# Two-block transformer kernel on one core: router's logits by token, halved refills, nine taps on TensorE, postponed GpSimd products

## The reference, cut to what matters

```python
def conv_mixer(...):                       # layer 0 of the first block
    u = x @ w_in; a_val, a_gate, b_b, b_c, b_x = split(u)
    a = a_val * sigmoid(a_gate)
    a = causal_depthwise_conv(a, a_dw) + a_dw_b      # 31 taps, 512 channels
    a = silu(layer_norm(a, ...))
    ...
def route(xf, w_router, b_router):         # 16 experts in 4 groups
    logits = xf @ w_router + b_router
    probs = softmax(logits)                # best group, its two best experts, their gates
def moe(x, ...):                           # in layers 0 and 1 of the first block
    # each token goes to 2 of 16 experts: silu(x@w1[e]) * (x@w3[e]) @ w2[e]
# first block, each layer: x = layer_norm(ALPHA*x + mixer(x)); x = layer_norm(ALPHA*x + moe(x))
# second block: forgetting attention, ffn with a conv, dilated attention, ffn, rms_norm
```

## Time and profile before

| | us |
|---|---|
| median of 3 runs | 1748.67 |
| lowest, highest | 1748.58, 1749.48 |
| the profiled execution | 1751.06 |
| its span, first to last instruction | 1749.8 |
| PE, DVE, ACT, POOL busy | 1701.1, 791.5, 625.8, 131.2 |
| TensorE's mean granted clock | 0.999 |

### The profile page before, as it was taken

One profiled execution on the slowest core, in us unless ns is written; L12 is line 12 of the kernel. 1 busy time (PEld: TensorE's weight loads), 2 busy tenths in 40 slices (PEclk: granted clock), 3 DMA queues, 4 the chain that ended last, 5 costly groups with the idle time before them and its releaser, 6 DMA issues.

```text
span 1749.8 us, 23960 instructions
## 1 busy us (share of the span) xinstructions
PE 1701.1 (97%) x9986; PEld 1114.9 (64%) x9986; DVE 791.5 (45%) x1520; ACT 625.8 (36%) x1203; POOL 131.2 (7%) x152
## 2 busy tenths in 40 slices
PE   9999999999899999999999989999999999999998
PEld 8974344433334984344343333887999899789997
DVE  6971111111103792111111012866888677868885
ACT  5541110000002670100010002666666564756665
POOL 0000000000001000000000001331111011301101
PEclk9999999999999999999999999999999999999999
DMA  9869999999999799999999999534555544435550
GB/s 380 331 241 401 422 429 428 428 427 428 426 425 419 291 377 393 424 428 430 428 427 427 426 424 420 190 124 144 172 191 183 202 161 154 141 137 171 191 193 24
DMA packets 56947, 544.88 MB, mean 311 GB/s; under 512 B 6400, under 2 KB 6400, under 8 KB 8832
## 3 DMA queue, kind: packets, MB, share of 16 engines
q1 hardware_dynamic: 56416, 542.14, 76.8%
q10 hardware_dynamic: 416, 1.13, 0.2%
HBM read 542.19 MB, written 1.05 MB: 310 GB/s over the span
## 4 chain that ended last, share of the span: by engine, by line
PE 75%; DMA 20%; DVE 4%; ACT 1%; POOL 0%; issue 0%; SPq 0%; ACTq 0%; DVEq 0%
PE PS L1313 22%; DMA ring<-in_w 20%; PE PS L440 13%; PE PS L442 13%; PE PS L441 13%; PE PS L1367 2%; PE PS L1295 2%; PE PS L1513 2%; PE PS L1021 1%; PE PS L2056 1%; PE PS L1329 1%; DVE wl L411 1%; PE PS L1381 1%; PE PS L1486 1%; DVE sm L650 0%; PE PS L2937 0%
## 5 line engine op out<-in xcount | busy, mean ns | idle before, releaser
L1313 PE MATMUL PS<-ring,F 128*64 128x512 f32 x1984 | 444.3, 595 | 26.2 <-DMA ring<-in_w 22.1
L411 DVE TENSOR_TENSOR wl<-ring,wh 128x512 fp32r<-128x512 f32 x496 | 359.3, 741 | 143.3 <-ACT wh L405 140.9
L405 ACT ACTIVATE wh<-ring 128x512 fp32r<-128x512 f32 x504 | 315.0, 630 | 267.8 <-PE PS L442 245.1
L1313 PEld LDWEIGHTS PS<-ring,F 128*64 128x64 f32 x1984 | 140.3, 137 | 306.9 <-issue 264.5
L440 PE MATMUL PS<-xh,wl 128*128 128x256 f32 x1128 | 325.2, 288 | 0.1
L441 PE MATMUL PS<-xl,wh 128*128 128x256 f32 x1128 | 319.2, 283 | 0.0
L442 PE MATMUL PS<-xh,wh 128*128 128x256 f32 x1128 | 319.2, 283 | 0.0
L440 PEld LDWEIGHTS PS<-xh,wl 128*128 128x128 f32 x1128 | 216.3, 192 | 2.7 <-DVE wl L411 0.9
L441 PEld LDWEIGHTS PS<-xl,wh 128*128 128x128 f32 x1128 | 216.4, 192 | 0.7
L442 PEld LDWEIGHTS PS<-xh,wh 128*128 128x128 f32 x1128 | 216.4, 192 | 0.0
L440 PE MATMUL PS<-wh,xl 128*128 128x512 f32 x320 | 129.7, 405 | 0.2 <-DVE F L2597 0.2
(11 more groups left out here) (451 smaller groups left out, 2056.5 us busy)
## 6 DMA issues: line engine op xcount, KB each, us to landing
ring<-in_w SPq DMA_DIRECT2D x98, 2048.0 KB, 25.6
ring<-in_w SPq DMA_DIRECT2D x68, 1024.0 KB, 12.2
ring<-in_ffn_up SPq DMA_DIRECT2D x44, 1024.0 KB, 4.9
early<-in_w SPq DMA_DIRECT2D x16, 2048.0 KB, 26.7
F<-in_w SPq DMA_DIRECT2D x15, 2048.0 KB, 26.5
F<-in_w SPq DMA_DIRECT2D x22, 1024.0 KB, 10.7
ring<-in_ffn_down SPq DMA_DIRECT2D x22, 1024.0 KB, 4.9
ZX<-in_w SPq DMA_DIRECT2D x7, 2048.0 KB, 26.8
```

The lines of the kernel that those rows point to most:

```text
L405: act.e.activation(self.wh[:, p % NPIECE, :], self.piece_source(p), ACT.Copy).then_inc(*self.up("w_hi", p))
L411: dve.e.tensor_tensor(self.wl[:, p % NPIECE, :], self.piece_source(p), f32(self.wh[:, p % NPIECE, :]), ALU.subtract).then_inc(*self.up("w_ ...
L1313: t = pe.e.matmul(PS[64 * half:64 * half + 64, bank, :], lhs(k), weights[:, a:a + 512], start=(k == 0), stop=(k == 7))
```

## The change

- Router: the logits are made with tokens on partitions, [128 x 16] for each half, in banks 0 and 1, with x as the stationary operand; the bias comes in as a product of a row of ones with `brow`. VectorE's additions and TensorE's transposes of the logits go; `TURN_ORDER` becomes (2, 3, 0, 1).
- The first three refills of experts' places in each layer (chunks 24 to 26) go as two loads of 512 KB: the first waits for half of the products of the chunk that was there (`expert_half`), the second for all of them.
- GpSimd's products with the last norm's gain are of 512 columns; the second and the later ones wait until `xl` is complete. VectorE's additions and some steps of the forget gate move by a slot or two.
- `PE_TAPS` is 9: 36 instead of 44 convolution products; the first tap of VectorE's part is made by ScalarE, without the bias, which the last sum adds; `steps` is new.
- x is loaded whole before the first weights; the first block is made like the others.

```diff
-PE_TAPS = 11
+PE_TAPS = 9
+HALVED = {CHUNK[f"moe{layer}"] + 24 + i: layer for layer in range(2) for i in range(3)}
@@ class Kernel
+    def half_landed(self, n):
+        return [(self.s_last, 48 + 64 * HALVED[n])] if n in HALVED else []
-    TURN_ORDER = (1, 2, 3, 0)
+    TURN_ORDER = (2, 3, 0, 1)
@@ def sync_load
+            if n in HALVED:
+                sp.wait_ge(self.at("expert_half", PREVIOUS[n]))
+                sp.e.dma_start(self.chunk(n)[:, 0:1024], src[:, 0:1024]).then_inc(self.s_last, 16)
+                sp.wait_ge(self.released(PREVIOUS[n]))
+                sp.e.dma_start(self.chunk(n)[:, 1024:2048], src[:, 1024:2048]).then_inc(self.ring_sems[SLOT[n]], 16)
+                continue
@@ def sync_setup
-        for j, pieces in enumerate((slice(0, 512), slice(512, 1024))):
+        for j in range(2):
             columns = slice(512 * j, 512 * j + 512)
             self.sp.e.dma_start(self.X[:, :, columns], x[:, :, columns]).then_inc(self.x_in[j][0], 16)
+        for j, pieces in enumerate((slice(0, 512), slice(512, 1024), slice(1024, 2048))):
             self.sp.e.dma_start(self.chunk(0)[:, pieces], self.source(0)[:, pieces]).then_inc(self.first_in[j][0], 16)
-        pieces = slice(1024, 2048)
-        self.sp.e.dma_start(self.chunk(0)[:, pieces], self.source(0)[:, pieces]).then_inc(self.first_in[2][0], 16)
@@ def even_tensor
-            for _ in self.tensor_features("ev", p + 4 * c, (6, 1, 2, 3, 4, 5, 0, 1, 4, 5)[c], c == 0):
-                for _ in range(0 if c < 3 or c > 8 else 1 if c == 8 else 2):
+            for _ in self.tensor_features("ev", p + 4 * c, (6, 1, 2, 3, 4, 5, 0, 1, 4, 5)[c]):
+                for _ in range(0 if c < 3 or c > 7 else 1 if c == 7 else 2):
@@ def even_scalar
+                for ch in {(2, 0): (0, 1), (4, 0): (2, 3)}.get((c, j), ()):
+                    act.wait_ge(at("ev_dve", 1 + 2 * (ch // 2)), at("ev_pad"))
+                    act.e.activation(v["acc"][:, ch, :], v["aP"][:, ch, PE_TAPS:PE_TAPS + 256], ACT.Copy,
+                                     scale=v["aw"][:, ch, PE_TAPS:PE_TAPS + 1]).then_inc(*up("ev_first_tap", ch))
@@ def even_vector: all four low parts of x, then the splits; in convolve
-                if k == PE_TAPS:
-                    dve.wait_ge(at("ev_dve", 1 + 2 * (c // 2)))
-                    t = dve.e.tensor_scalar(acc[:, c, :], src, wk, v["b2"][:, c:c + 1], ALU.mult, ALU.add)
-                else:
...
+                dve.wait_ge(at("ev_first_tap", c) if k == PE_TAPS + 1 else at("ev_tap", c, k - 1))
+                dve.e.scalar_tensor_tensor(out=acc[:, c, :], in0=src, scalar=wk, in1=acc[:, c, :], op0=ALU.mult,
+                                           op1=ALU.add).then_inc(*up("ev_tap", c, k))
-                 (2, 3): [(convolve, 1)], (3, 3): [(convolve, 3), (value, 1)], (5, 3): [(convolve, 2), (product, 0)],
...
+                 (2, 3): [(convolve, 2)], (3, 3): [(convolve, 2), (value, 1)], (5, 3): [(convolve, 2), (product, 0)],
+                 (6, 3): [(convolve_b, 0)], (7, 0): [(convolve, 3)], (7, 1): [(convolve, 3)], (7, 2): [(convolve, 3)],
+                 (7, 3): [(convolve, 1), (product, 1)], (8, 0): [(convolve, 2)], (8, 1): [(convolve, 2)],
+                 (8, 2): [(convolve_b, 1)], (8, 3): [(gate_b, 0)], (9, 0): [(convolve, 2)], (9, 1): [(convolve, 1)],
+                 (9, 2): [(convolve, 2)], (9, 3): [(gate_b, 1)]}
-                for step, n in steps.get((c, j), [(convolve, 4 if (c, j) in ((4, 1), (5, 1), (6, 1)) else 3)] if c > 2 else []):
+                for step, n in steps.get((c, j), [(convolve, 4)] if c > 2 else []):
-            dve.e.tensor_tensor(acc[:, c, :], acc[:, c, :], PS[:, 6 + c // 2, c % 2 * 256:c % 2 * 256 + 256],
-                                ALU.add).then_inc(*up("ev_sum", c))
+            dve.e.scalar_tensor_tensor(out=acc[:, c, :], in0=acc[:, c, :], scalar=v["b2"][:, c:c + 1],
+                                       in1=PS[:, 6 + c // 2, c % 2 * 256:c % 2 * 256 + 256], op0=ALU.add,
+                                       op1=ALU.add).then_inc(*up("ev_sum", c))
@@ router
     def logits_of(self, h):
-        return self.PS[64 * h:64 * h + 16, 2 * h, 0:128]
+        return self.PS[:, h, 0:16]
@@ def tensor_logits
+        if k == 0:
+            pe.wait_ge(self.br_in, self.at("consts", "ones"))
+            pe.e.matmul(self.logits_of(h), self.ones[0:1, 0:128], self.brow[:, :], start=True, stop=False)
-        t = pe.e.matmul(self.logits_of(h), wr[:, k, :], self.RT[:, k, h * 128:h * 128 + 128], start=k == 0, stop=k == 7)
+        t = pe.e.matmul(self.logits_of(h), self.RT[:, k, h * 128:h * 128 + 128], wr[:, k, :], start=False, stop=k == 7)
@@ def moe_tensor_route
-        frees = [[at("logits_t", layer, 0)], [], [at("logits_t", layer, 1)], []]
-        self.tensor_to_tokens(layer, self.RT, ready, frees, order[:1])
-        for h in range(2):
-            r = slice(64 * h, 64 * h + 16)
-            pe.wait_ge(at("logits_t", layer, h))
-            t = pe.e.transpose(PS[:, 6 + h, 0:16], self.lgT[r, :], self.ident[r, r])
-        t.then_inc(*up("logits_turned", layer))
-        self.tensor_to_tokens(layer, self.RT, ready, frees, order[1:])
+        frees = [[at("logits_less_max", layer)], [], [], []]
+        self.tensor_to_tokens(layer, self.RT, ready, frees, order)
@@ def tensor_first_product
+                    if kk == 0 and (c, ex) in ((0, 0), (0, 1), (1, 0)):
+                        t.then_inc(*self.up("expert_half", n))
@@ forget, TensorE, ScalarE and VectorE: the spread of rms, its copy and the gate's logits
-            if s == -3:
+            if s == -2:
@@ def forget_vector
-            if s in (-8, -7):
-                h = s + 8
-                dve.wait_ge(at("x_gain", h))
+            if s in (-8, -6):
+                h = (s + 8) // 2
+                dve.wait_ge(at("x_gain", h, 1))
                 e.tensor_tensor(self.X[:, h, :], self.X[:, h, :], self.last_rows()[:, 1, :], ALU.add).then_inc(
                    *up("x_final", h))
@@ def forget_pool
         for h in range(2):
-            pool.wait_ge((self.s_row, 32), self.half_normed("moe1", h, 0), self.half_normed("moe1", h, 1))
-            e.tensor_tensor(self.X[:, h, :], self.Z[:, h, :], self.last_rows()[:, 0, :], ALU.mult).then_inc(*up("x_gain", h))
+            for d in range(2):
+                columns = slice(512 * d, 512 * d + 512)
+                pool.wait_ge((self.s_row, 32), self.half_normed("moe1", h, d))
+                if (h, d) == (0, 1):
+                    pool.wait_ge(at("x_lo", "fg", 3))
+                e.tensor_tensor(self.X[:, h, columns], self.Z[:, h, columns], self.last_rows()[:, 0, columns],
+                                ALU.mult).then_inc(*up("x_gain", h, d))
```

More of the change, by code:

```diff
@@ L76 @@
     ("ev_ready", "ev_consts ev_pad"), ("norm_stats", "stats moments var_eps less_mean"),
-    ("norm_scale", "rstd shift"), ("route", "logits_t logits_less_max route chosen ranks_read"),
+    ("norm_scale", "rstd shift"), ("route", "logits_less_max route chosen ranks_read"),
     ("gating", "gating gate_slots counts_read overflow_flag"),
-    ("routed", "logits logits_turned ranked counted"),
+    ("routed", "logits ranked counted expert_half"),
     ("od_recur", "od_rate od_gating od_gated od_input od_state od_join"),
@@ L380, in sync_load @@
                     sp.wait_ge(self.released(PREVIOUS[m]))
-            src = self.source(n)
             if n in LAST_CHUNKS:
@@ L449, in tensor_busy @@
             self.pe.e.matmul(self.PS[:, bank, 0:256], self.ident[:, :], self.ones[:, :], start=True, stop=True)
-    def tensor_first_features(self, stage, p, out, xh, xl):
-        pe = self.pe
-        for k in range(8):
-            h, l = self.weight(p + k // 4)
-            a = slice(k % 4 * 128, k % 4 * 128 + 128)
-            pe.wait_ge(self.at("x_hi", stage, k // 2), self.low_made(p + k // 4))
-            pe.e.matmul(out, l[:, a], xh[:, k, :], start=k == 0, stop=False)
-            pe.e.matmul(out, h[:, a], xh[:, k, :], start=False, stop=False)
-        for k in range(8):
-            h, l = self.weight(p + k // 4)
-            a = slice(k % 4 * 128, k % 4 * 128 + 128)
-            pe.wait_ge(self.at("x_lo", stage, k // 2))
-            t = pe.e.matmul(out, h[:, a], xl[:, k, :], start=False, stop=k == 7)
-            if k % 4 == 3:
-                t.then_inc(*self.up("w_used", p + k // 4))
-                yield p + k // 4
     def first_chunk(self, stage):
@@ L531, in tensor_first_normed_chunk, with tensor_features @@
         low(3)
-    def tensor_features(self, stage, p, bank, first=False):
+    def tensor_features(self, stage, p, bank):
         pe, PS = self.pe, self.PS
@@ L537, in tensor_features @@
         for j in range(2):
-            if first and j == 0:
-                yield from self.tensor_first_features(stage, p, PS[:, bank, 0:256], xh, xl)
-                continue
             for k in range(8):
@@ L1062, in high @@
```

(38 more changed lines are left out.)

28 lines of the change are left out of this document (9 added, 19 removed).

## The result

The changed kernel takes 1754.54 us (median of 7 runs, 1753.14 to 1756.08) where the kernel before takes 1748.99 (7 runs): a ratio of 1.0032, 95% interval 1.0022 to 1.0041. It is slower by 0.3%; the prediction was 1744.4 us, faster. The mean granted clock of the profiled execution is 0.991 in place of 0.999; it took 1754.19 us (span 1752.9).

The account below looks back on a forecast made before the run. Experts' DMAs bound each layer, started by TensorE's first releases; after 1080 us TensorE's chain counts. Terms -3.3 + 0.5 + 0.55 - 0.9 - 0.3 - 0.8 = -4.3 us took the median from 1748.67 to 1744.4, range 1740.5 to 1747.2.

Parts of the forecast that it names:

- part 3: Router, logits by token: products and transposes at their new pace, +0.55 us in layer 0, bounds -0.8 and +0.8.
- It costs nothing there: Router of layer 1: the longer router is free, as DMAs run without a break from 628 to 660 us.
- Part 5: Forget stage, GpSimd's products wait: low parts of x come sooner, a later split waits; -0.8 us, bounds -0.3 and -2.1.
- four slots of 1.44 us in hand: Forget stage: the steps moved by one slot were said to have this much room.
- Part 4: Experts, first three refills in halves: -0.9 us in layer 0, -0.3 in layer 1 (bounds +0.5 and -2.5).
- Part 1: Mixer of layer 0, nine taps on TensorE: 36 convolution products for 44, VectorE just in time; -3.3 us, bounds 0 and +1.5 on VectorE's lateness.
- Part 2: Start of the kernel, x loaded before the first weights: +0.5 us, bounds -0.5 and +0.9.
- D: Rival for the halved refills: each half pays 2.5 us fixed cost, 15 us in all, 1759.4 us; chance 0.04.

Follow-up runs that it names:

- e5: Changed kernel with the router's logits' products 64 columns wide instead of 16 and the bias product second; 1748.6 us, ratio 0.9998 to the kernel before.
- e2: Changed kernel with the forget-stage change undone (GpSimd's products whole and without the wait, steps in old slots); 1753.9 us, ratio 1.0030 to the kernel before.
- e4: Changed kernel with the three refills loaded in one piece again; 1754.9 us, ratio 1.0031 to the kernel before.
- e6: Kernel before with only the router's logits by token added, 16 columns wide; 1754.8 us, ratio 1.0035.
- e13: Kernel before with only the router's logits by token added, products 64 columns wide; 1750.6 us, ratio 1.0006.
- e8: e3 plus the forget stage's steps in their new slots, GpSimd's products where they were before; 1747.6 us, ratio 0.9993 to the kernel before.
- e7: e3 plus GpSimd's postponed products, the forget stage's steps in their old slots; 1746.8 us, ratio 0.9989 to the kernel before.
- e12: e3 with GpSimd's two products of X with a row made by VectorE instead; 1745.7 us, ratio 0.9977 to the kernel before.
- e11: Kernel before with only the nine convolution taps on TensorE (11 before); 1745.7 us, ratio 0.9979.
- e1: Changed kernel with the router's logits by expert again, the rest kept; 1747.3 us, ratio 0.9986 to the kernel before.
- e3: Changed kernel with both the router change and the forget-stage change undone; 1746.3 us, ratio 0.9982 to the kernel before.
- e9: Kernel before with only nine taps on TensorE and x loaded before the first weights; 1746.6 us, ratio 0.9985.
- e10: Kernel before with only the three refills in halves; 1750.3 us, ratio 1.0001.

## Why the prediction was wrong

**The step that failed is part 3's.** It priced the new logits by instructions at full clock, and that price was good: in e5 the pace was 0.118 us for the 0.11 of the estimate, 16 transposes took 1.75 (1.75 to 1.8 forecast), the filler 1.73 (1.7), and A grew by 0.6 us where the sum had +0.55. What the step lacked was a term for TensorE's clock. The table before the prediction gave the mean clock as 0.999 and no row of the kernel before shows a fall in a router; the step left the clock there when it changed the products under it. With 16 columns a product it was 1.2 GHz in both routers of each of the four kernels that have them (the changed one, e2, e4, e6); with 64 columns or the logits by expert it was 2.4 GHz in both routers of all the others. The term's size: 1.4 to 3.0 us in A, 1.4 to 3.1 in B. With it the router grew by 3.6 us in A where the sum had 0.55; by the ratios part 3 cost 6.1 us with the fall (e6) and 1.0 without (e13).

"It costs nothing there", for layer 1, held for the slip that the forecast had in mind and not for the one that came. With wide products B is 0.6 us longer and C is 433.7 and 433.9, inside the 433.1 to 434.6 of all kernels at full clock there. With half clock B is 2.1 to 3.7 us longer and C is 435.2 to 436.7; from e13 to e6 both grow by 1.5, so nothing of that is hidden. The rows show full DMAs to 660 us, and it was inferred that they would stay so whatever the router took. But the first refill of before was issued at 661.3 with the last of the 24 chunks landing at 663.4: 2.1 us in hand, where a refill needs 4.6 to land (5.0 in layer 0). And that last chunk waits for the router too: it is issued behind the turns back to tokens, at 655.1 us before and 657.0 in the changed kernel.

**Part 5** was put at -0.8 and is +0.4, +2.0 with the half clock. The low parts gained 2.6 us up to the end of the first block, and the wait of about 1 us for a split was foreseen (1.2). The step ended there. It didn't follow VectorE's delay on through the sum, the rms and the spread to the gate and the keys, where another 1.4 us are due: "four slots of 1.44 us in hand" was an assertion from TensorE's side. e8 refutes it, as the moved slots alone make TensorE wait 1.1 us and the stage 0.6 longer, and e7 and e12 show that the chain that fills the slots is VectorE's. It quoted the rule of the Trainium skill, SBUF — State Buffer, "SBUF: two separate sides", that VectorE and GpSimd lock each other out. The trace agrees: the sum took 2.31 us beside GpSimd's products and 1.21 without them.

**Part 4** was put at -1.2 and the ratio is 1.0001 (0.9992 to 1.0010). The earlier issue was worth its 0.9 us for four chunks and nothing at the end. Of its bounds for layer 0, 0 and -2.5, the upper was right.

**Part 1** held: -3.3 forecast, the mean's products 3.3 us sooner and -3.7 by e11's ratio. VectorE was in time: its last four sums take from 86.53 to 88.20 and TensorE's mean begins at 88.69 (88.7 and 88.6 were worked out), and its idle time for high parts from 20 to 92 us fell from 9.1 to
```profile
L421 DVE TENSOR_TENSOR wl<-ring,wh 128x512 fp32r<-128x512 f32 x38 | 26.3, 695 | 4.1 <-ACT wh L415 4.0
```
**Part 2**, +0.5 with bounds -0.5 and +0.9: +0.3 on the average of the profiles, so it held; that the changed kernel's own profile began 0.2 us sooner was luck of that execution.

None of the rivals was this one. D, the slower case, had a price for the halves that the runs refute, and slower as a whole had a chance of 0.05. A forecast could have had it as one. The Trainium skill, TensorE: Matmul & The Clock Gate, "HAM oscillation — how this bites in real kernels", tells of a matmul kernel with thin M (128) whose clock drops again and again, and advises to change the loop or pad M. It blames the waits for DMAs between the products; in the trace here TensorE was busy 2.00 us of 2.00 when the clock fell, so on the cause the measurement and the page differ, while wider products were the cure here too.

What stays open: by the ratios the parts alone give -3.7 (e11), +6.1 (e6), +0.7 for part 5 (e1 less e3), +1.0 for part 2 (e9 less e11) and +0.2 (e10), 4.3 us in all for 5.6 measured, with intervals of 1.5 us and more on each term. The profiles carry noise of the same size: from the first gather to layer 1's turn the sixteen of them took 518.0 to 520.4 us, in no order of the parts. Why products of few columns lose the clock while TensorE is busy isn't shown, only that they do and that the wide form cures it; the place of the bias product, which e5 and e13 change with the width, wasn't tried alone.

## What to carry to other kernels

Before you swap the operands of a small product so that its few columns move and a full 128x128 stands, look at the granted clock and give the edit a term for it; if the product has to be so, widen it with columns that nobody reads and compare. Where an edit delays a step that "DMAs hide", subtract the time at which the first refill is issued from the landing of the last chunk in the queue: that is the cover, 2.1 us here for a refill that needs 4.6; then ask whether the edit delays that last chunk as well. And when an engine's stall goes, follow the engine that was late to its next three consumers, not to its next one.

## What the runs showed of the hardware

- The granted clock went from 2.4 to 1.2 GHz in or just behind a run of products of 16 moving columns, with a full 128x128 as stationary operand, though TensorE was busy 2.00 us of 2.00 there; with 64 columns it stayed at 2.4 GHz, and an instruction took no longer (0.118 us, against 0.116 for the 24 of 2.78 us in layer 1).
- A stretch of 3.4 us at half clock cost the router 1.4 to 1.5 us and the forget stage 1.7, one of 6.8 us cost the router 3.0 to 3.1.
- The fall reached past its cause: in e6 the logits were done at 123.3 us at full clock, and the transposes and the filler behind them paid.
- The same waits in the forget stage (1.2 and 1.4 us) were followed by half clock in three kernels and by full clock in another (e5).
- A product of 1024 columns that GpSimd makes in 2.8 us takes VectorE 1.21 us, and no low part waits for it.
